# A state-space scan with the logarithm of its time step in the decay sums, two masked exponentials added, and its matmuls spread over a slot

## The reference, cut to what matters

```python
dt = softplus(dt_raw + dt_bias)                      # (S, 2, G, R): both directions
a_dt = dt * a                                        # a = -exp(a_log)
a_cs = cumsum(a_dt)                                  # within a chunk of 128
xdt = x * dt[..., None]
decay = exp(where(tril, a_cs[l] - a_cs[s], -inf))    # 128 x 128 per head and chunk
cb = einsum('bclgn,bcsgn->bcgls', c, b)
y_diag = einsum('bcgls,bcgrls,bcsgrp->bclgrp', cb, decay, xdt)
states = einsum('bclgn,bcgrl,bclgrp->bcgrpn', b, exp(a_cs[-1] - a_cs), xdt)
y_off = einsum('bclgn,bcgrpn,bcgrl->bclgrp', c, prev, exp(a_cs))
y = y_fwd + y_bwd + x * d_skip                       # then gated by silu(z), normed by group
```

## Time and profile before

| | |
|---|---|
| median of 3 runs | 1014.03 us (1012.89 to 1016.27) |
| profiled execution, its span | 1017.87 us, 1016.0 us |
| TensorE matmul busy | 958.5 us, 94% |
| VectorE, ScalarE, GpSimd busy | 661.3, 521.9, 208.7 us |
| TensorE's mean granted clock | 0.968 |
| chain that ended last | PE 74%, DVE 12%, POOL 6%, issue 5% |

### The profile page before, as it was taken

How to read it: one execution, slowest core, us unless ns; L and a number is a source line. 1 busy time by engine, 2 the same in 40 slices (tenths; PEclk the granted TensorE clock), 3 DMA queues, 4 the chain that set the end, 5 groups by cost and what they waited for, 6 DMA issues and landing times.

```text
span 1016.0 us, 13856 instructions
## 1 busy us (share of the span) xinstructions
PE 958.5 (94%) x5758; PEld 846.3 (83%) x5758; DVE 661.3 (65%) x746; ACT 521.9 (51%) x660; POOL 208.7 (21%) x184
## 2 busy tenths in 40 slices
PE   5998998897988999998999999899999999999998
PEld 4997887876776788888999888689978789999887
DVE  4378985968898966467666444675864766665442
ACT  5457894463663563346555433555554355545331
POOL 0005665768787000000000000430000000000000
PEclk9999997898898999998999999899999999999999
DMA  8743232342221538543445555665336345555551
GB/s 311 267 167 108 100 119 89 125 165 63 84 83 77 193 124 323 185 181 136 171 166 194 198 189 207 156 217 176 129 129 230 125 169 205 194 186 202 179 194 42
DMA packets 24975, 166.56 MB, mean 164 GB/s; under 512 B 2938, under 2 KB 3066, under 8 KB 6224
## 3 DMA queue, kind: packets, MB, share of 16 engines
q1 hardware_dynamic: 22320, 156.12, 43.5%
q0 software_dynamic: 2592, 9.54, 3.3%
HBM read 164.57 MB, written 1.08 MB: 163 GB/s over the span
## 4 chain that ended last, share of the span: by engine, by line
PE 74%; DVE 12%; POOL 6%; issue 5%; ACT 2%; DMA 1%; SPq 0%; DVEq 0%; ACTq 0%; POOLq 0%
PE ps L345 67%; POOL conv_acc L1675 2%; PE ps L529 2%; POOL y_off L1673 2%; DVE step_w L1298 2%; DVE conv_acc L1258 2%; PE ps L427 1%; DVE w_lo L1084 1%; POOL logit L1662 1%; DVE decay L1303 1%; DVE xtok L1279 1%; DMA raw<-in_w_stream 1%; DVE xtok L1335 1%; DVE gates L1365 1%; DVE gates L1362 1%
## 5 line engine op out<-in xcount | busy, mean ns | idle before, releaser
L1084 DVE TENSOR_TENSOR w_lo<-raw,w_hi 128x2048 fp32r<-128x2048 f32 (+1 forms) x147 | 340.8, 2323 | 225.1 <-ACT w_hi L750 225.1
L750 ACT ACTIVATE w_hi<-raw 128x2048 fp32r<-128x2048 f32 (+1 forms) x147 | 279.6, 1903 | 214.8 <-PE ps L345 213.6
L345 PE MATMUL ps<-ht_hi,w_hi 128*128 128x256 f32 x952 | 274.9, 289 | 3.1 <-DVE ht_lo L1122 2.9
L345 PE MATMUL ps<-ht_lo,w_hi 128*128 128x256 f32 x952 | 272.7, 286 | 0.0
L345 PE MATMUL ps<-ht_hi,w_lo 128*128 128x256 f32 x952 | 272.4, 286 | 0.0
L345 PEld LDWEIGHTS ps<-ht_hi,w_hi 128*128 128x128 f32 x952 | 185.9, 195 | 6.2 <-DVE ht_lo L1122 3.5
L345 PEld LDWEIGHTS ps<-ht_lo,w_hi 128*128 128x128 f32 x952 | 185.9, 195 | 0.0
L345 PEld LDWEIGHTS ps<-ht_hi,w_lo 128*128 128x128 f32 x952 | 185.7, 195 | 0.0
L345 PE MATMUL ps<-w_hi,ht_hi 128*128 128x512 f32 (+1 forms) x320 | 126.5, 395 | 0.2 <-issue 0.2
L345 PE MATMUL ps<-w_hi,ht_lo 128*128 128x512 f32 (+1 forms) x320 | 123.7, 387 | 0.0
L345 PE MATMUL ps<-w_lo,ht_hi 128*128 128x512 f32 (+1 forms) x320 | 123.6, 386 | 0.0
(11 more groups left out here) (231 smaller groups left out, 1234.8 us busy)
## 6 DMA issues: line engine op xcount, KB each, us to landing
raw<-in_w_stream SPq DMA_DIRECT2D x146, 1024.0 KB, 4.8
bias<-rel_scratch POOLq DMA_DIRECT2D x1, 3072.0 KB, 15.1
bias<-in_rpb POOLq DMA_DIRECT2D x16, 128.0 KB, 4.6
gates<-in_gate_bias POOLq DMA_DIRECT2D x2, 768.0 KB, 5.3
x_first<-in_x_in SPq DMA_DIRECT2D x2, 512.0 KB, 4.0
x<-in_x_in POOLq DMA_DIRECT2D x1, 1024.0 KB, 6.3
g_post<-in_post POOLq DMA_DIRECT2D x2, 512.0 KB, 8.9
out_y<-x SPq DMA_DIRECT2D x4, 256.0 KB, 2.0
```

The source lines that it names most:

```text
L345: ins = pe.matmul(o, still, moving, start=first and n == 0, stop=last and n == 2, skip_group_check=True)
L750: act.activation(w_hi[s % SPLIT_RING][:, 0:width(s)], raw[s % RAW_RING][:, 0:width(s)], ACT.Copy).then_inc(hi_ready, 1)
L1084: dve.tensor_tensor(w_lo[s % SPLIT_RING][:, 0:width(s)], raw[s % RAW_RING][:, 0:width(s)], w_hi[s % SPLIT_RING][:, 0:width(s)].bitcast(F32 ...
```

## The change

The decay's exponent gets log(dt[s]) added, so that exp gives decay times dt and no step weights are needed. `minus_log_dt` makes -log(dt) on VectorE from exponent and mantissa with a series, right behind softplus; `cumulate` adds it to the sums of the source tokens by four more matmuls. The lesser of two no longer works with such a term, so each direction is masked instead: a matmul of `unit` with `far` (-1e30 in the wrong triangle) adds to each decay bank, ScalarE takes the exponential of both banks straight from PSUM, and VectorE adds the two and multiplies by cb, chunk by chunk. GpSimd's step_weights goes; it makes `unit` and `far` once. The decays get two buffers, and the diagonal of a group moves one slot on. On TensorE decay(s-26, 1), states(s-27), diagonal(s-27) and across(s-27) now stand between the two halves of slot s's stream; cb(s-25) and decay(s-25, 0) stay behind it. On ScalarE and VectorE the group's work moves one slot on as well; ScalarE's z Silu now follows it. The dt slot moves from 6 to 4, ahead of kv, and with it its transposition, softplus and logarithm (VectorE's slot 6). Cut to its core:

```diff
-S_KV = 4
-S_DT = 6
+S_DT = 4
+S_KV = 5
...
-        decay = [at(f"decay{i}", [P, PER_GROUP, P], 141376 + 2048 * i) for i in range(2)]
-        step_w = [at(f"step_w{i}", [P, PER_GROUP, P], 145472 + 2048 * i) for i in range(3)]
-        step_tmp = at("step_tmp", [P, PER_GROUP, P], 151616)
+        decay = [[at(f"decay{i}_{c}", [P, PER_GROUP, P], 141376 + 4096 * i + 2048 * c) for c in range(RT)]
+                 for i in range(2)]
+        decay_back = [at(f"decay_back{c}", [P, PER_GROUP, P], 149568 + 2048 * c) for c in range(RT)]
         cb = at("cb", [P, RT, P], 153664)
+        far = at("far", [P, 2, P], 154688, F32R)
+        ndt = at("ndt", [P, RT, 2 * HEADS], 158272)
+        unit = at("unit", [P, P], 158784, F32R)
...
+        ndt_wide = at("ndt_wide", [P, 4, 4, HEADS], 184160)
...
+                    if half == 0 and between:
+                        between(s)
...
                 pe.wait_ge(cum_s_ready, g + 1)
-                for d in (1, 0):
+                if g == 0 and c == 0:
+                    pe.wait_ge(far_ready, 1)
+                for d in range(2):
                     key = ("decay", g, c, d)
                     claim(key, 5 + d)
                     pe.matmul(ps[:, 5 + d, :], cum_s[g % 2][:, 2 * c + d, :], cum_l[c][:, d, :, :],
-                              start=True, stop=True).then_inc(*fill_of(key))
+                              start=True, stop=False)
+                    pe.matmul(ps[:, 5 + d, :], unit[:, :], far[:, d].unsqueeze(1).to_broadcast([P, PER_GROUP, P]),
+                              start=False, stop=True).then_inc(*fill_of(key))
...
                 for u in range(4):
-                    ins = pe.matmul(ps[:, 5, u * P:u * P + P], adt_wide[:, u].rearrange("p q h -> p (q h)"),
-                                    tri[:, u % 2], start=True, stop=True)
+                    pe.matmul(ps[:, 5, u * P:u * P + P], adt_wide[:, u].rearrange("p q h -> p (q h)"),
+                              tri[:, u % 2], start=True, stop=False)
+                    ins = pe.matmul(ps[:, 5, u * P:u * P + P], ndt_wide[:, u].rearrange("p q h -> p (q h)"),
+                                    ident, start=False, stop=True)
...
+            def ssd_between(s):
+                if 0 <= s - 26 < GROUPS:
+                    ssd_decay(s - 26, 1)
+                if 0 <= s - 27 < GROUPS:
+                    ssd_states(s - 27)
+                    ssd_diagonal(s - 27)
+                    ssd_across(s - 27)
...
-                stream(s)
+                stream(s, ssd_between)
...
                     ssd_cb(s - 25)
-                if 0 <= s - 26 < GROUPS:
-                    ssd_diagonal(s - 26)
-                if 0 <= s - 25 < GROUPS:
                     ssd_decay(s - 25, 0)
-                if 0 <= s - 26 < GROUPS:
-                    ssd_states(s - 26)
-                if 0 <= s - 25 < GROUPS:
-                    ssd_decay(s - 25, 1)
-                if 0 <= s - 26 < GROUPS:
-                    ssd_across(s - 26)
                 if 36 <= s < 40:
...
-            def backward_sums(g, c):
-                if g:
-                    ready(act, ("y", g - 1))
-                key = ("decay", g, c, 1)
-                ready(act, key)
-                act.activation(decay[c][:, :, :], ps[:, 6, :].rearrange("p (h l) -> p h l", h=PER_GROUP),
-                               ACT.Copy).then_inc(*drain_of(key))
+            def decay_exps(g, c):
+                for d, dest in enumerate((decay[g % 2][c], decay_back[c])):
+                    key = ("decay", g, c, d)
+                    ready(act, key)
+                    if d == 0 and g >= 2:
+                        ready(act, ("y", g - 2))
+                    if d == 1 and g:
+                        act.wait_ge(decay_scaled, 2 * g - 1 + c)
+                    act.activation(dest[:, :, :], ps[:, 5 + d, :].rearrange("p (h l) -> p h l", h=PER_GROUP),
+                                   ACT.Exp).then_inc(*drain_of(key))
...
+                if 0 <= s - 28 < GROUPS:
+                    g = s - 28
+                    act.wait_ge(gated, g + 1)
+                    for c in range(RT):
+                        if g or c:
+                            act.wait_ge(gsq_ready, 2 * g + c)
+                        act.activation(junk[:, :], xtok[:, c, g * GW:g * GW + GW], ACT.Square,
+                                       accum_out=gstat[:, 0, 2 * g + c:2 * g + c + 1]).then_inc(gsq_ready, 1)
+                if 0 <= s - 26 < GROUPS:
+                    g = s - 26
+                    key = ("cb", g)
+                    ready(act, key)
+                    if g:
+                        act.wait_ge(decay_scaled, 2 * g)
+                    act.activation(cb[:, :, :], ps[:, 7, 0:2 * P].rearrange("p (c l) -> p c l", c=2),
+                                   ACT.Copy).then_inc(*drain_of(key))
+                    decay_exps(g, 0)
+                    decay_exps(g, 1)
+                if 0 <= s - 27 < GROUPS:
+                    key = ("state", s - 27)
+                    ready(act, key)
+                    act.activation(state[:, :, :], ps[:, 7, :].rearrange("p (a b) -> p a b", a=2),
+                                   ACT.Copy).then_inc(*drain_of(key))
                 if name == "z" and closes:
...
+            def minus_log_dt():
+                bits = dt[:, :, :].bitcast(I32)
+                e, f, m, z, w, p = (dtw[:, i] for i in range(6))
+                link(dve.tensor_scalar(e.bitcast(I32), bits, 23, None, ALU.logical_shift_right))
+                link(dve.tensor_scalar(m.bitcast(I32), bits, 0x007FFFFF, 0x3F800000, ALU.bitwise_and,
+                                       ALU.bitwise_or))
+                link(dve.tensor_copy(f, e.bitcast(I32)))
+                link(dve.tensor_scalar(f, f, 127.0, -math.log(2.0), ALU.subtract, ALU.mult))
+                link(dve.tensor_scalar(w, m, 1.0, None, ALU.add))
+                link(dve.reciprocal(z, w))
+                link(dve.scalar_tensor_tensor(z, m, 1.0, z, ALU.subtract, ALU.mult))
+                link(dve.tensor_tensor(w, z, z, ALU.mult))
+                link(dve.tensor_scalar(p, w, 1.0 / (2 * LOG1P_TERMS + 1), None, ALU.mult))
+                for k in range(LOG1P_TERMS - 1, 0, -1):
+                    link(dve.scalar_tensor_tensor(p, p, 1.0 / (2 * k + 1), w, ALU.add, ALU.mult))
+                link(dve.scalar_tensor_tensor(p, p, 1.0, z, ALU.add, ALU.mult))
+                dve.scalar_tensor_tensor(ndt[:, :, :], p, -2.0, f, ALU.mult, ALU.add).then_inc(ndt_ready, 1)
...
+            def ssd_weigh(g, c):
+                emptied(dve, ("decay", g, c, 0)), emptied(dve, ("decay", g, c, 1))
+                w = decay[g % 2][c]
+                link(dve.tensor_tensor(w[:, :, :], w[:, :, :], decay_back[c][:, :, :], ALU.add))
+                if c == 0:
+                    emptied(dve, ("cb", g))
+                dve.tensor_tensor(w[:, :, :], w[:, :, :],
+                                  cb[:, c, :].unsqueeze(1).to_broadcast([P, PER_GROUP, P]),
+                                  ALU.mult).then_inc(decay_scaled, 1)
...
-            def ssd_lesser(g, c):
-                key = ("decay", g, c, 0)
-                ready(dve, key)
-                emptied(dve, ("decay", g, c, 1))
-                dve.tensor_tensor(decay[c][:, :, :], ps[:, 5, :].rearrange("p (h l) -> p h l", h=PER_GROUP),
-                                  decay[c][:, :, :], ALU.min).then_inc(*drain_of(key))
-            def ssd_weigh(g):
-                emptied(dve, ("cb", g))
-                dve.wait_ge(step_w_ready, 2 * (g + 1))
-                for c in range(RT):
-                    w = step_w[(2 * g + c) % 3]
-                    ins = dve.tensor_tensor(w[:, :, :], w[:, :, :],
-                                            cb[:, c, :].unsqueeze(1).to_broadcast([P, PER_GROUP, P]), ALU.mult)
-                link(ins)
-                for c in range(RT):
-                    dve.wait_ge(decay_ready, 2 * g + c + 1)
-                    dve.tensor_tensor(decay[c][:, :, :], decay[c][:, :, :], step_w[(2 * g + c) % 3][:, :, :],
-                                      ALU.mult).then_inc(decay_scaled, 1)
...
+                    minus_log_dt()
...
-                    ssd_lesser(s - 25, 0)
                 if 0 <= s - 26 < GROUPS:
-                    ssd_skip(s - 26)
-                if 0 <= s - 25 < GROUPS:
-                    ssd_lesser(s - 25, 1)
+                    ssd_weigh(s - 26, 0)
+                if 0 <= s - 27 < GROUPS:
+                    ssd_gate(s - 27)
                 if 0 <= s - 26 < GROUPS:
-                    ssd_gate(s - 26)
-                if 0 <= s - 25 < GROUPS:
-                    ssd_weigh(s - 25)
+                    ssd_weigh(s - 26, 1)
                 if name == "gate" and closes:
...
-            def step_weights(g):
-                for c in range(RT):
-                    i = 2 * g + c
-                    if i >= 3:
-                        pool.wait_ge(decay_scaled, i - 2)
```

(12 more changed lines are left out.)

86 lines of the change are left out of this document (29 added, 57 removed).

## The result

| | before | after |
|---|---|---|
| median of the runs shown together, us | 1014.35 (1012.89 to 1016.27) | 998.25 (996.91 to 999.05) |
| ratio, 95% interval | | 0.9836 (0.9811 to 0.986) |
| profiled execution, us; its span | 1017.87; 1016.0 | 997.53; 995.7 |
| GpSimd's second softmax multiply, us | 82.45 | 84.43 |
| first cb to end of slot 34, us | 124.0 | 103.45 |

Forecast were 1002.3 us, in a range of 991 to 1011, with "faster" as the likeliest sign.

A forecast was written before the change was run, and what follows sets the result against it. Before the scan VectorE's unbroken queue, in the scan VectorE filled by contention with GpSimd's step weights, bound the kernel. Scan gain 17.0 less 3.5, 1.5 and 0.3 gives 11.7 us off the median 1014.03: 1002.3 us, range 991 to 1011.

The forecast's parts named there:

- the full slots: Scan, slots 27 to 33: seven slots set by TensorE at 11.8 us each, 82.6 us.
- the table waits: Scan, slots 27, 29, 31: TensorE waits for exponentials behind ScalarE's table load, 1.5 us plus 0.6 for the clock, 6.3 altogether.
- slot 26: First slot of the scan: cb, two decay groups, a stream and 0.4 for `far`, 9.0 us.
- 6.4 less 4.5: Slots 27, 29, 31: ScalarE needs 6.4 us to the exponentials, TensorE arrives after 4.5; wait taken as some 1.5.
- the term for `far`: Slot 26: 0.4 us for the mask, which GpSimd makes after the convolution's last Silu.
- The logarithm: Before the scan: 18 linked VectorE operations, 6.0 us, in a queue without gaps; shift and mask taken at 0.22 each.
- The net delay of the second softmax multiply: Before the scan: VectorE's queue, with logarithm and moved dt slot, ends 3.5 us later; bounds 1.5 and 6.5.
- The 1.8 taken for the sums: Before the scan: four more `cumulate` matmuls cost 1.5 us, their wider copies 0.3.
- Contention in part (1007.9): Scan: GpSimd's `x_state` and `cum_s` still lengthen VectorE's slot to 11.6 us; net gain 6.1, 1007.9 us; chance 0.20.
- The wait in every slot (1032): Scan: late ScalarE idles TensorE mid-slot every time, its clock falls, 17.0 us a slot; 1032 us; chance 0.10.
- The better case (994): Front loses only 1.5 us and nothing waits at the tables: 20 us less, 994; chance 0.12.
- the matmuls only move the wait: Scan: the wait moves from diagonal to states, slots near 14.4 us, within 3 us of 1014; chance 0.08.

The follow-up runs named there:

- x3: Changed kernel with GpSimd's six step-weight operations a slot put back as load into memory nobody reads: 1020.06 us.
- b1: Kernel before without GpSimd's step weights (buffers filled with ones), its order kept: 986.29 us, ratio 0.9729.
- m1: Changed kernel without the four mask matmuls a group, exponents scaled down to stay finite: 994.91 us.
- c1: Changed kernel with ScalarE's Silu of z one slot later and the table of Exp loaded ahead directly behind it: 992.75 us.
- c2: Changed kernel with GpSimd's multiply that makes the mask `far` moved from the start of the scan to slot 20: 995.23 us.
- x1: Changed kernel with the logarithm left out and its place filled with zeros: 991.04 us.
- b2: Kernel before with only the dt slot moved from 6 to 4, k and v to slots 5 and 6: 1010.01 us.
- all three edits: Changed kernel with z's Silu a slot later and Exp's table loaded ahead, the mask made in slot 20, the logarithm in slots 15 and 17: 985.27 us.

## Why the prediction was right

Its mechanism held: GpSimd's step weights filled VectorE, and without them TensorE sets the pace of a slot. 11.7 us less were worked out, and the medians lie 16.1 apart. The size came as near as it did because errors cancelled in part: in the scan the full slots (3.5 us) and the table waits (1.9 with the starts behind them) were taken too long, slot 26 too short (1.8).

*The scan's slots.* Forecast 107.0 us, measured 103.45. Full slots: seven of 11.8, 82.6 us; they were 11.33, about 79. The mask matmuls come every 0.23 us, not 0.27, which is 0.16 of the 0.47 a slot. The rest is TensorE's other work, taken at 10.92 less 0.2 for the ends of matmuls ahead of waits; 11.33 less four times 0.23 leaves 10.4. VectorE's 9.4 us a slot were 8.5 and `w_lo` 2.29, as forecast from the rows without GpSimd. Contention as the cause was argued from two rows there; x3 and b1 show it.

*The waits for the table.* Right in place, releaser and number. They were 0.65, 1.59 and 1.59 us, 3.8 in all, where 6.3 were taken, 1.8 of it for a fall of the clock that didn't come: L537 takes 1.90 us right behind the wait. That was luck in part, since in m1 one of two equal waits brought it. The forecast's own terms, 6.4 less 4.5, give 1.9 us a wait and not the 1.5 that it took. c1 shows the cause.

*Slot 26.* 9.0 forecast, 10.8 measured: the term for `far` was 0.4 and is 2.9 (c2), a wait of 1.15 us and the low clock behind it. The rest of the slot was taken at 8.6 and is 7.9. This is the one place in the scan where the term was too small.

*The front.* The logarithm takes from 60.40 to 66.50 us in the trace of after, 6.1 us for the 6.0 worked out, shift and mask at 0.22 and 0.23 as taken. The net delay of the second softmax multiply was 2.0 us, not 3.5. The medians split the front as -3.5 for the move and +7.2 for the logarithm, 3.7 together. The 1.8 taken for the sums isn't shown by itself: F of x1 is 1.4 longer than that of b2, but F differs by up to 3.1 us between executions whose front is the same. With the 1.4 the loss is 5.1, for which the forecast had 5.3; by F of b1, whose front is that of before, it is 3.5. That the profile of after starts its scan only 0.3 us later is no contradiction: the profiled execution of before was itself late in the front, by its clock. F of before and of b1:

```profile
61.33:221.16 159.83, 144.97 (x1052) 130.85 (x1051) 134.62 (x221) 107.70 (x188) 90.13 (x73) 0.94 0.34 117
```

```profile
59.51:216.22 156.71, 141.84 (x1051) 127.87 (x1051) 134.86 (x221) 107.75 (x188) 90.33 (x73) 0.97 0.35 120
```

*The sum.* Gain in the scan 20.6 for 17.0, loss in front 3.5 to 5 for 5.3: 15.5 to 17 us by the runs, 16.1 measured.

*The rivals.* Contention in part (1007.9) fell: GpSimd's `x_state` and `cum_s` still run, and VectorE's slot is 8.5 us. The wait in every slot (1032) fell, though its premise was sound: m1 shows that ScalarE is ready only 0.1 us ahead (0.46 us of masks ahead of the pair less the 0.33 that its start is late without them). It decided from 14.4 us a slot on, and the longest is 13.14. The better case (994) didn't come: the table waits are there until c1's edit takes them out, and the log isn't hidden. That the matmuls only move the wait, with slots near 14.4 (within 3 us of 1014), fell too: a full slot is 11.33 with no wait in it.

The Trainium skill's page "ScalarE: Activation LUTs", section "Step-by-step: what each stage is for", puts a table load at about 2.7 us with its drain; the trace of after shows 1.28, and the next operation right behind it. Its page "SBUF — State Buffer", section "Who interferes with whom", says that a VectorE operation with two SBUF inputs contends with a GpSimd operation that reads SBUF. The traces agree: in x3 the sum of two SBUF operands is 0.71 us alone and 1.22 beside the load, and L1328, with one of its inputs in PSUM, is 0.68 in both.

## What to carry to other kernels

An engine off the critical path can set the time by what it does to its neighbour. Hold the duration of the same instruction with and without the other at work before counting operations: here 15 to 28 us hung on it. Small work in a queue without gaps costs its full length where the chain runs through that queue (7 us for 6.1 of logarithm), and a few slots later nothing that shows in the time; so look for the place first. And leaving work out of the bound engine pays only down to the next engine: of 0.93 us a slot 0.33 came.

## What the runs showed of the hardware

The logarithm's operations in slot 6 take 0.22 to 0.29 us each, but for the reciprocal (0.95). In slot 15, beside GpSimd, most of them are longer. VectorE and then GpSimd with all three edits:

```profile
141.09 1.91 DVE L1270 TENSOR_SCALAR dtw<-dt 128x128 int32<-128x128 int32 x1
143.03 0.41 DVE L1272 CAST dtw<-dtw 128x128 f32<-128x128 int32 x1
```

```profile
141.02 1.89 POOL L1673 TENSOR_TENSOR logit<-logit,soft 128x1024 f32<-128x1024 f32 x1 [6.88 <-DVE soft L1232]
142.89 0.93 POOL L1684 TENSOR_SCALAR y_off<-conv_in,params 128x256 f32<-128x256 f32 x1
```

An operation of one input, 0.23 us by itself, took 1.91 and ended 0.09 us behind GpSimd's multiply of 1.89, which began just ahead of it. So it isn't only operations with two inputs that are held up.

Behind a wait of 1.59 us in mid-scan TensorE's clock stayed at full; behind 1.15 us in slot 26, which comes shortly after another wait of 1.05, it was at 0.50 and the matmuls took 0.63 us for 0.40. Without the mask matmuls it fell behind a wait of 2.03 us in slot 29 (0.88 over the slot) and stayed full behind one of 2.03 in slot 31. The length of the last wait alone doesn't tell which it will be.
